# One weight load of expert 30 issued as 33 transfers instead of one

## What is computed

```python
def moe_ffn(h, w_router, b_router, w_gate_up, b_gate_up, w_down, b_down):
    ...
    for e in range(N_EXPERTS):                       # 32
        gu = t @ w_gate_up[e] + b_gate_up[e]         # (256,1024) @ (1024,2048)
        g, u = gu[:, :D_EXPERT], gu[:, D_EXPERT:]
        g = jnp.minimum(g, SWIGLU_LIMIT)
        u = jnp.clip(u, -SWIGLU_LIMIT, SWIGLU_LIMIT)
        act = (u + 1) * (g * jax.nn.sigmoid(SWIGLU_ALPHA * g))
        y = act @ w_down[e] + b_down[e]              # (256,1024) @ (1024,1024)
        out = out + combine[:, e:e + 1].astype(t.dtype) * y
    return out.reshape(B, S, D)
```

## Time and profile before

| | us |
|---|---|
| median of three runs | 1165.8 |
| lowest and highest run | 1165.79, 1166.43 |
| the profiled execution's own time | 1165.2 |
| its span, from the first to the last instruction | 1163.5 |
| PE busy | 1133.3 |
| DVE busy | 302.1 |
| ACT busy | 182.7 |

### The profile page before, as it was taken

The page is one execution under the profiler, slowest core; times in us unless marked ns, Lnnn a source line. Parts: engine busy times, 40 slices in busy tenths (PEclk is TensorE's granted clock), DMA queues, the critical chain, the costliest instruction groups (busy, mean ns, idle before and its releaser), DMA issues.

```text
span 1163.5 us, 13811 instructions
## 1 busy us (share of the span) xinstructions
PE 1133.3 (97%) x5632; PEld 576.4 (50%) x5632; DVE 302.1 (26%) x790; ACT 182.7 (16%) x391; POOL 11.5 (1%) x26
## 2 busy tenths in 40 slices
PE   9999999999999999999999999999999999989997
PEld 7888888734344443434343344443434343433346
DVE  0549943411113122111111212121111111111126
ACT  1214220212121211111011011111111111101012
POOL 0020000000000000000000000000000000000000
PEclk9999999999999999999999999999999999999999
DMA  9975357699999999999999999999999999999971
GB/s 360 383 280 217 138 233 317 266 361 429 428 425 425 437 430 430 426 431 431 431 427 430 430 419 437 431 430 430 430 432 431 429 428 432 430 432 423 424 332 38
DMA packets 37420, 447.15 MB, mean 384 GB/s; under 512 B 3200, under 2 KB 6304, under 8 KB 19296
## 3 DMA queue, kind: packets, MB, share of 16 engines
q1 hardware_dynamic: 32752, 439.79, 89.9%
q10 hardware_dynamic: 4592, 6.33, 1.5%
HBM read 443.49 MB, written 2.62 MB: 383 GB/s over the span
## 4 chain that ended last, share of the span: by engine, by line
PE 81%; DMA 14%; DVE 3%; issue 1%; SPq 0%; ACT 0%; DVEq 0%; ACTq 0%
PE bank L483 49%; DMA arena<-in_w_gu 13%; PE bank L802 10%; PE bank L454 5%; PE bank L502 3%; PE bank L954 2%; PE bank L967 2%; PE bank L1389 2%; PE bank L489 2%; DMA arena<-in_w_in 1%; PE bank L836 1%; DVE arena L522 1%; PE bank L878 1%; PE bank L477 1%; DVE arena L542 0%
## 5 line engine op out<-in xcount | busy, mean ns | idle before, releaser
L483 PE MATMUL bank<-arena 128*64 128x512 f32 x3168 | 694.3, 594 | 15.1 <-DMA arena<-in_w_gu 10.5
L483 PEld LDWEIGHTS bank<-arena 128*64 128x64 f32 x3168 | 235.7, 137 | 436.8 <-issue 406.6
L522 DVE TENSOR_TENSOR arena<-bank,arena 128x512 f32<-128x512 f32 x32 | 22.1, 692 | 657.0 <-PE bank L489 656.9
L802 PE MATMUL bank<-arena 128*128 128x256 f32 x512 | 112.7, 380 | 0.0
L802 PEld LDWEIGHTS bank<-arena 128*128 128x128 f32 x512 | 96.6, 190 | 14.2 <-issue 1.3
L1554 ACT ACTIVATE arena<-bank 128x512 f32<-128x512 f32 x31 | 18.5, 597 | 361.0 <-PE bank L483 361.0
L502 PE MATMUL bank<-arena 64*128 64x512 f32 x272 | 67.8, 616 | 0.8 <-ACT arena L1561 0.7
L454 PEld LDWEIGHTS bank<-sel,arena 128*128 128x128 f32 x480 | 54.7, 192 | 11.4 <-issue 11.4
L454 PE MATMUL bank<-sel,arena 128*128 128x128 f32 x480 | 57.6, 278 | 0.0
L1561 ACT ACTIVATE arena<-bank 128x512 f32<-128x512 f32 x32 | 19.1, 597 | 214.8 <-PE bank L483 214.8
L1778 DVE SCALAR_TENSOR_TENSOR arena<-arena 128x256 f32<-128x256 f32 x120 | 48.5, 479 | 0.5 <-DVE arena L1778 0.2
(11 more groups left out here) (223 smaller groups left out, 522.6 us busy)
## 6 DMA issues: line engine op xcount, KB each, us to landing
arena<-in_w_gu SPq DMA_DIRECT2D x47, 4096.0 KB, 32.2
arena<-in_w_dn SPq DMA_DIRECT2D x23, 4096.0 KB, 31.9
arena<-in_w_gu SPq DMA_DIRECT2D x27, 2048.0 KB, 15.4
arena<-in_w_dn SPq DMA_DIRECT2D x14, 2048.0 KB, 16.2
arena<-in_w_in SPq DMA_DIRECT2D x17, 1024.0 KB, 17.5
arena<-in_w_gu SPq DMA_DIRECT2D x13, 1024.0 KB, 8.2
arena<-in_w_dn SPq DMA_DIRECT2D x8, 1024.0 KB, 6.7
arena<-in_w_out SPq DMA_DIRECT2D x4, 1024.0 KB, 4.8
```

The costliest lines, as they stand in the source:

```text
L483: mm = pe.matmul(to[half * CAP:(half + 1) * CAP, :], rows, w[:, half * 512:(half + 1) * 512], start=first, stop=last)
L522: nc.vector.tensor_tensor(by_bias(gt, 8), by_bias(of_gate[:, :], 8), bias_of(e, 0, 0, 8), ALU.add).then_inc(sw_step, 1)
L802: mm = pe.matmul(bank[n % 4][:, lo:S], w[:, k, j * P:(j + 1) * P], xT_sb[:, k, lo:S], start=(k == 0), stop=(k == KD - 1))
```

## The change

The load of expert 30's first gate and up weights is issued as 33 transfers. The first 512 of the 4096 columns are loaded in 16 groups of partitions, of 1, 2, 3, ... 15 and 8 partitions, which make 128. Each group is loaded by two transfers: group i (from 0) takes its columns 0 to 16(i+1) in one and the columns from there to 512 in the other. The last transfer takes the columns 512 to 4096 of all 128 partitions. The bytes and where they go are the same. All 33 count on the semaphore of the load's place, and PE waits for 33 times 16.

```diff
         JOINED = [n for n in JOINED if place_of(n + 1) == place_of(n) + 1]
+        IN_PARTS = load_no(NE - 2, 0)
+        GROUPS = [*range(1, 16), 8]
         counts, arrival = [0] * ES, []
@@
-                counts[slot_no[n]] += 16 * PIECES.get(n, 1)
+                counts[slot_no[n]] += 16 * (2 * len(GROUPS) + 1 if n == IN_PARTS else PIECES.get(n, 1))
                 arrival.append((slot_no[n], counts[slot_no[n]]))
@@ load_pair
+            if n == IN_PARTS:
+                to, of = slot_of(n), w_gu[e, c // 2 * 512:(c // 2 + 1) * 512, :].rearrange("(p r) d -> p (r d)", r=4)
+                of = of[:, c % 2 * PAIR:(c % 2 + 1) * PAIR]
+                at = 0
+                for i, size in enumerate(GROUPS):
+                    ps = slice(at, at + size)
+                    cut = 16 * (i + 1)
+                    sp.dma_start(to[ps, 0:cut], of[ps, 0:cut]).then_inc(e_in[slot_no[n]], 16)
+                    sp.dma_start(to[ps, cut:512], of[ps, cut:512]).then_inc(e_in[slot_no[n]], 16)
+                    at += size
+                sp.dma_start(to[:, 512:PAIR], of[:, 512:PAIR]).then_inc(e_in[slot_no[n]], 16)
+                return
```

## The result

| | before | after |
|---|---|---|
| median | 1165.86 us (8 runs, 1164.76 to 1166.61) | 1168.7 us (8 runs, 1168.19 to 1171.6) |
| the profiled execution | 1165.2 | 1168.2 |
| its span | 1163.5 | 1166.5 |

After against before is a ratio of 1.0025, with a 95% interval of 1.0016 to 1.0034. So the change costs 2.8 us (1.9 to 4.0). The forecast was 0.9 us, with a range up to 1173: the way in which the delay reaches the end was right, and its size three times too small. The forecast's own range, to 1168, was missed by 0.7 us; the wider one held.

A forecast was written before the change was run, and what follows sets the result against it. PE and the DMA engines were near their limits, with PE waiting for queued expert loads. Issue 0 plus 0.9 us for packets and unequal shares, on 1165.8, gave 1166.7 us; own range 1165.6 to 1168, 8-in-10 range 1165.0 to 1173.

The forecast's parts named there:

- What bounds the kernel: PE and DMA near their limits; PE waits 1.28 us for expert 31's third load, so added queue time reaches the end.
- d: Time the change adds to the DMA engines' work through their queue, passed on to PE's end; forecast 0.9 us.
- 6.7 us of room: Changed load lands at 1065.0, PE comes to it at 1071.70, so PE does not wait for this load itself.
- rival 2: Small transfers cost more than their packets, about 5 us, 1171 us; sign: landing after 1069 with full DMA share; chance 0.13.
- Part 1, the issue: On SP: 33 issues at 0.50 us end at 1041.5, hidden by the DMA backlog until 1060.1; cost 0.
- the margin to 1060.1: SP done issuing 18.6 us before the last joined load lands at 1060.1, so the engines never run dry.
- Part 2, the packets: DMA queue: 256 small pieces and as many completion marks at 12 ns over 16 engines; 0.4 us taken, upper bound 3.2.
- the row of 32 partitions at 221 us: Two 64 KB transfers landing 0.1 to 0.2 us apart, taken to bound a transfer's own cost at about 0.1 us.
- Part 3, the unequal shares: DMA engines: small pieces may load one engine more; 0.9 us taken between 0.4 (even) and 1.4, at the worst 9.1.
- Rival 1: Queue takes only about nine transfers, so the DMA engines run dry after 1060; about 13.5 us, 1179 us; chance 0.13.
- Rival 3: The latest DMA engine gets 16 KB less, 0.6 us, which PE's idle time lets through; 1165.2 us; chance 0.07.
- Rival 4: Each small transfer waits for the one before, 2.0 us each, 64 us for 32; 1230 us; chance 0.01.

The follow-up runs named there:

- e3: Against the kernel before: whole load in 32 transfers of 32 partitions 4 apart by 512 columns, no wide transfer; 1166.96 us, ratio 1.0008.
- e10: Against the kernel before: 32 transfers of 32 partitions by 512 columns, written 4 apart, read from HBM rows side by side; 1166.89 us, ratio 1.0009.
- e4: The changed kernel with its 16 groups uncut, 17 transfers; 1167.72 us, ratio 1.0015 to the kernel before.
- e12: The changed kernel with every group cut at column 256, all small pieces 1024 bytes; 1168.4 us, ratio 1.0026 to the kernel before.
- e5: The changed kernel with each group's partitions 4 apart instead of side by side; 1168.85 us, ratio 1.0024 to the kernel before.
- e7: Against the kernel before: first 512 columns in transfers of 127 partitions and of 1, then the wide one; 1172.63 us, ratio 1.0055.
- e8: Against the kernel before: first 1024 columns in transfers of 108 and 20 partitions, then the wide one; 1170.32 us, ratio 1.0041.
- e2: Against the kernel before: whole load in 32 transfers of 16 partitions 8 apart by 1024 columns; 1173.74 us, ratio 1.0067.
- e11: Against the kernel before: 32 transfers of 32 partitions by 512 columns, written side by side, read from HBM rows 4 apart; 1174.13 us, ratio 1.0074.
- e9: Against the kernel before: 32 transfers of 32 partitions by 512 columns, side by side in writes and reads; 1175.12 us, ratio 1.0079.
- e6: Against the kernel before: 32 transfers of 16 partitions by 1024 columns, written side by side, read from HBM rows 8 apart; 1175.28 us, ratio 1.0079.
- e1: Against the kernel before: whole load in 32 transfers of 16 adjacent partitions by 1024 columns, no wide transfer; 1178.83 us, ratio 1.0101.

## Why the prediction was right in its way and short in its size

The packet records in one table. "Foreign" is how many KB an engine writes outside its own partitions, by the Trainium skill's table, its pattern scaled down for 32 partitions, and one row after the other for up to 16.

```
kernel                      foreign KB   loss us   loss/16   over before (median)
e3  32 rows, 4 apart                0        18       1.1           1.3
e10 32 rows, 4 apart                0        18       1.1           1.3
e4  groups uncut                  222        24       1.5           2.1
change                            222        43       2.7           2.8
e12 cut in the middle             222        44       2.8           2.8
e5  groups 4 apart                224        43       2.7           2.9
e7  127 and 1                     240        42       2.6           6.6 (one engine)
e8  108 and 20                    468        61       3.8           4.3
e2  16 rows, 8 apart             1792       138       8.6           8.1
e11 32 side by side              1920       128       8.0           8.5
e9  32 side by side              1920       152       9.5           9.5
e6  16 side by side              1920       165      10.3           9.3
e1  16 side by side              1920       202      12.6          13.2
```

The change's 2.7 less the 0.2 of the kernel before, and 0.2 us for its additional packets (below), make 2.7, against 2.8 measured. e7 aside, loss/16 stands within about 1 us of what was measured in every row.

- **What bounds the kernel: right.** d passes to the end one to one. One detail was off. PE's wait before expert 31's third load did not grow from 1.28 to 2.2: it is 1.29. The delay was taken in three waits ahead of it (0.23, 0.30 and 1.24 us), because those loads had become late too. The changed load had 6.7 us of room. It landed at 1068.7, later than the 1066 that the prediction gave it and just short of the 1069 that was to be rival 2's sign, and PE came to it at 1072.58 with no wait.
- **Part 1, the issue, at 0: right in the outcome.** An issue takes 0.34 us while SP is free. SP was held from the 27th transfer and done at 1048.6, not 1041.5; the margin to 1060.1 shrank and held. The share in the windows shows no hole.
- **Part 2, the packets: right for what it priced.** 512 at 7.3 ns and the bytes as before are 0.23 us, 0.4 was taken. The step took the row of 32 partitions at 221 us for a bound on all shapes. It is none: there the engines had next to nothing else to do, and it shows 0.1 us for a transfer in a free queue.
- **Part 3, the unequal shares, is the term that was mis-sized.** The mechanism is there: the small pieces lie on engines 0 to s - 1 of a transfer of s partitions. All 256 of them, told by their sizes, form unbroken rows of 32, 30, 28 ... down to 2 on 15 engines, and none on the sixteenth, as the Trainium skill's rule had it that the prediction set beside its own value. Which of the 16 these are the records do not say; here they go by the rule as 0 to 14. But it added nothing. Engine 0 reached its small pieces at 1053.6 us and engine 12, the last, at 1061.5, so the heavily loaded engine was far from the latest, which got 2 to 6 small pieces. So the 0.5 us that part 3 put on top of the 0.4 were not there, and about 2.5 us of slow packets stood in their place.
- **Rival 2 is where those 2.5 us come from**: "small transfers cost more than their packets", and its words on "few partitions that many engines write at once" were near. It had 0.13 and 5 us. Of the change's 43 us, 13 are in the small pieces, nearly all in those behind an engine's fourteenth, and 29 in packets of 14 KB and more. For these F, that it matters whose partitions are written, is an argument from e1 to e3 and e9 to e11: no run gave the change's own groups to the engines whose partitions they are. That the wider range took in 1168.7 is owed to this rival, not to the terms of the sum.
- **Rival 1 did not come.** SP had 26 small transfers and joined loads out before it was held. Its hole is seen faintly in e3 and e10 (shares of 0.89 and 0.87) and more in e7.
- **Rival 3** was tried by itself in e8. No gain showed; if there was one, it was buried under the same cost. **Rival 4** did not come: 32 transfers cost 1.3 to 2.8 us in e3 and the change, so the 2.0 us of the earlier trace rows overlap.

Not shown: that two engines at one port of SBUF is what slows them. It fits most of the runs, and the write side is shown for 32 partitions, but no record names a partition or a port, and how 32 or 108 partitions are dealt out over the engines is assumed. Why a foreign KB costs 0.17 to 0.20 us of engine time in the change, e5, e7 and e12, but 0.07 to 0.13 in the others, stays open as well (1 KB alone takes 0.038), and so does e6, which came out 4 us below e1 with the same writes.

No version ran faster than the kernel before. Of those that cut the load, e3 and e10 are the only ones that can't be told from it.

## What to carry to other kernels

In a kernel that waits for its DMA queue, the number of transfers is cheap as long as old work covers the issue: 32 cost about 1 us here. The shape is what costs: load into all 128 partitions at once, as the kernel before does. A cut along the columns alone was not timed. Where partitions must be split, 32 of them with a step of 4 cost 1.3 us, hardly to be told from nothing, while 32 side by side cost 9.5. Read the rate beside the share: share and rate down together is an empty queue, and a full share with the rate down is slow packets.

## What the runs showed of the hardware that was not expected

- Where a transfer writes changes the pace of the others in the queue: in e8, 32 KB packets that the edit did not touch lost 19 us in all.
- The 16 DMA engines were up to 7.8 us apart in the same queue (1053.6 to 1061.5 us at the same transfers). So what is added to one engine costs nothing until it is the latest: 13.0 us of small pieces on engine 0 cost 6.6.
- What holds SP is what is outstanding on one engine: one transfer with 127 row pieces on one engine held the next issue for 30 us, and 26 transfers with few on each did not.
- In the change an engine runs 14 pieces of under 2 KB at full pace (4 ns lost each in the mean), and each one behind them takes 95 to 175 ns more; e5 and e12 have as many slow pieces.
- An issue of a transfer of few partitions takes 0.23 to 0.37 us, hardly less than the 0.33 of one of 128.
